# Two more weight slots for the start of a routed expert loop, half of expert 0 ahead of the rest of the gather, and the second group gathered in later units

## What is computed

```python
scores = jax.nn.sigmoid((h @ router_w).astype(f32))
...
gate = jnp.sum(jax.nn.one_hot(top_idx, N_EXPERTS, dtype=f32) * top_w[..., None], axis=1)
...
for e in range(N_EXPERTS):
    he = jax.nn.silu(h @ w_gate[e]) * (h @ w_up[e])
    out = out + gate[:, e:e + 1] * (he @ w_down[e])
```

## Time and profile before

| | |
|---|---|
| median of 3 runs | 921.3 us (921.23 to 923.97) |
| the profiled execution, its own time | 920.35 us |
| its span, first to last instruction | 918.6 us |
| TensorE busy | 816.6 us, 89% of the span |
| VectorE, ScalarE busy | 322.3 us (35%), 181.7 us (20%) |
| mean granted TensorE clock | 0.96 of full speed |
| moved by DMA | 245.87 MB, mean 268 GB/s |

### The profile page before, as it was taken

One profiled execution on the slowest core, in us unless ns is written; L12 is line 12 of the kernel. 1 busy time (PEld: TensorE's weight loads), 2 busy tenths in 40 slices (PEclk: granted clock), 3 DMA queues, 4 the chain that ended last, 5 costly groups with the idle time before them and its releaser, 6 DMA issues. The chain is left out here.

```text
span 918.6 us, 12776 instructions
## 1 busy us (share of the span) xinstructions
PE 816.6 (89%) x5333; PEld 461.7 (50%) x5333; DVE 322.3 (35%) x671; ACT 181.7 (20%) x380; POOL 26.0 (3%) x102
## 2 busy tenths in 40 slices
PE   4999999977999999879579999999599999997882
PEld 3888566535534443323268876654364443432331
DVE  0186456464211111111252964282821111111115
ACT  1143323322211110000121323231241111100001
POOL 7100000000000000000000000000000000000000
PEclk8999999987999999999979999999799999999997
DMA  9744300265899999999935432020858999999991
GB/s 287 270 150 164 128 20 4 89 248 189 351 411 421 421 421 421 421 421 420 393 102 182 155 122 93 2 92 1 366 209 348 423 422 421 421 421 422 419 383 50
DMA packets 54229, 245.87 MB, mean 268 GB/s; under 512 B 8356, under 2 KB 11280, under 8 KB 29584
## 3 DMA queue, kind: packets, MB, share of 16 engines
q1 hardware_dynamic: 49824, 239.41, 65.4%
q0 software_dynamic: 1344, 4.72, 1.5%
q10 hardware_dynamic: 2992, 0.79, 0.4%
HBM read 243.85 MB, written 1.05 MB: 267 GB/s over the span
## 5 line engine op out<-in xcount | busy, mean ns | idle before, releaser
L906 PE MATMUL bank<-x_cm,ring 128*128 128x256 f32 x576 | 130.4, 389 | 6.3 <-ACT x_cm L1878 5.4
L482 PE MATMUL bank<-ring,xg 128*64 128x512 f32 x544 | 124.3, 596 | 10.8 <-DMA ring<-in_exp_w_up 8.6
L482 PE MATMUL bank<-ring_more,xg 128*64 128x512 f32 x480 | 112.5, 611 | 16.5 <-DMA ring_more<-in_exp_w_up 14.5
L906 PEld LDWEIGHTS bank<-x_cm,ring 128*128 128x128 f32 x576 | 112.1, 196 | 23.8 <-ACT x_cm L1878 5.8
L512 PE MATMUL bank<-ring,x_cm 128*64 128x512 f32 x480 | 108.2, 592 | 0.0
L673 DVE TENSOR_TENSOR y_lo<-bank,y_hi 128x512 fp32r<-128x512 f32 x32 | 22.1, 691 | 223.3 <-ACT y_hi L605 223.3
L482 PEld LDWEIGHTS bank<-ring,xg 128*64 128x64 f32 x544 | 40.8, 137 | 78.8 <-issue 73.2
L482 PEld LDWEIGHTS bank<-ring_more,xg 128*64 128x64 f32 x480 | 35.4, 140 | 82.4 <-issue 81.7
L512 PEld LDWEIGHTS bank<-ring,x_cm 128*64 128x64 f32 x480 | 34.8, 137 | 67.2 <-issue 66.3
L605 ACT ACTIVATE y_hi<-bank 128x512 fp32r<-128x512 f32 x32 | 19.1, 598 | 196.2 <-PE bank L512 196.2
L913 PE MATMUL bank<-ring,x_cm 128*128 128x512 f32 x128 | 57.7, 599 | 0.0
(11 more groups left out here) (364 smaller groups left out, 876.7 us busy)
## 6 DMA issues: line engine op xcount, KB each, us to landing
ring<-in_exp_w_down SPq DMA_DIRECT2D x60, 1024.0 KB, 17.6
ring<-in_exp_w_gate SPq DMA_DIRECT2D x34, 1024.0 KB, 13.2
ring<-in_exp_w_up SPq DMA_DIRECT2D x34, 1024.0 KB, 15.3
ring_more<-in_exp_w_gate SPq DMA_DIRECT2D x30, 1024.0 KB, 15.2
ring_more<-in_exp_w_up SPq DMA_DIRECT2D x30, 1024.0 KB, 17.2
ring<-in_w_in SPq DMA_DIRECT2D x24, 1024.0 KB, 9.1
ring<-in_w_out SPq DMA_DIRECT2D x8, 1024.0 KB, 6.5
ring_more<-in_exp_w_down SPq DMA_DIRECT2D x4, 1024.0 KB, 22.4
```

Of the source, the lines that this page charges most:

```text
L482: m = T.matmul(b[SL * i:SL * i + SL, :], xg[g][:, 4 * h + k, cols], w[:, k, :], start=(h == 0 and k == 0), stop=(h == 1 and k == 3))
L906: m = T.matmul(out_, w[:, k, c:c + n], x_cm[:, k, :], start=(k == 0), stop=(k == KD - 1))
```

## The change

`xg[1]`, the gather buffer of the second group, is used as two more slots for weights (`ONCE` = 2) on the first pass round the slots: loads 12 and 13 of a layer, the two halves of expert 1's down matrix, go there. From load 14 on the cycle has its twelve slots again. The landing of these two is counted on an existing semaphore, `rows_loaded`. So that the buffer is free for weights until they are used, the second group is gathered in units 4 to 7, two blocks in each: one where the block stood, and one behind the down product. The slot gates and the pick matrix of the second group move to unit 4. At the start of the expert part only four gather blocks stand ahead of the first half of expert 0 (`first_half`), which is now outside the branch; the other four follow it. For four rounds (not run here) the second group's blocks all stand behind the last unit of a group.

```diff
+    ONCE = 2
...
+    seen, holds, at = [0] * (NSLOT + MORE + ONCE), [None] * (NSLOT + MORE + ONCE), 0
+    for n, (l, name, h, parts) in enumerate(loads):
+        if (name, h) == ("gate0", 0):
+            cycle = [(at + i) % NSLOT for i in range(NSLOT)] + [NSLOT + i for i in range(MORE + ONCE)]
+            at = 0
...
+        at = (at + 1) % len(cycle)
+        if at == 0 and len(cycle) > NSLOT + MORE:
+            cycle = cycle[:NSLOT + MORE]
+        seen[slot] += 16 * len(parts)
...
+        landed.append(seen[slot] if slot < NSLOT + MORE else 16 * (len(rows) + 1 + ONCE * (l + 1)))
...
         def slot_ap(slot):
+            if slot >= NSLOT + MORE:
+                h = slot - NSLOT - MORE
+                return xg[1][:, 4 * h:4 * h + 4, :]
...
+        def steps_of(n, rounds):
+
+            i = n % GU
+            if n + GU >= NE * rounds + i:
+                return (), ()
+            if rounds > 1:
+                return (), tuple(range(KD)) if i == GU - 1 else ()
+            return ((2 * i - KD,), (2 * i - KD + 1,)) if 2 * i >= KD else ((), ())
+
+        def gates_at(n, rounds):
+
+            return n + GU < NE * rounds + n % GU and n % GU == (GU // 2 if rounds == 1 else GU - 1)
...
+        def first_half(pe, l):
+
+            (wg, full_g), (wu, full_u) = slot_w(l, "gate0", 0), slot_w(l, "up0", 0)
+            pe.wait_ge(*full_g)
+            pe.wait_ge(*full_u)
+            for k in range(4):
+                pe.wait_ge(*done("s_first", l, k + 1))
+                for i, w in enumerate((wg, wu)):
+                    T.matmul(b_hid[0][SL * i:SL * i + SL, :], xg[0][:, k, 0:SL], w[:, k, :], start=(k == 0), stop=False)
...
-            pe.wait_ge(*done("s_first", l))
             if rounds == 1:
+                for k in range(4, KD):
+                    pe.wait_ge(*done("s_first", l, k - 3))
+                    inc(gather(k, bank[k % 4], release="t_wgu" if k == 4 else None), "t_first")
                 st.have(pe, "t_gather", GU)
...
-            hidden(0, 0)
...
+            if rounds == 1:
+                pe.wait_ge(*done("s_first", l))
...
-                if g * GU < N:
-                    if n % GU == 0:
+                for k in inside:
+                    if k == 0:
                         pe.wait_ge(*at("v_pick", g + 1))
-                    mark(gather(n % GU, b_hid[n % 2]), "t_gather")
-                    if n % GU == 0:
-                        pe.wait_ge(*at("v_gcol", g))
-                        slot_gates(g)
-                if n + 1 < N:
+                    mark(gather(k, b_hid[n % 2]), "t_gather")
+                    gathered += 1
+                if gates_at(n, rounds) and rounds == 1:
+                    pe.wait_ge(*at("v_gcol", g))
+                    slot_gates(g)
+                turn_of_group = bool(behind) and n % GU == GU - 1
+                if n + 1 < N and not turn_of_group:
                     hidden(n + 1, 0)
...
                 down(n)
+                for k in behind:
...
+                    if rounds == 1 or k > 1:
+                        pe.wait_ge(*at("s_xg", gathered - (rounds > 1)))
+                    mark(gather(k, b_hid[(n + (k if rounds > 1 else 0)) % 2]), "t_gather")
+                    gathered += 1
...
+                if turn_of_group:
+                    hidden(n + 1, 0)
...
-                for k in range(KD):
-                    if k >= 4:
-                        pe.wait_ge(*done("s_first", l, k - 3))
-                    inc(gather(k, bank[k % 4]), "t_first")
+                for k in range(4):
+                    inc(gather(k, bank[k]), "t_first")
+                first_half(pe, l)
                 two_ways(pe, l, lambda rounds: experts_t(pe, l, rounds))
```

More of the change, by code:

```diff
@@ L102, in hybrid_trunk @@
     index = {(l, name, h): n for n, (l, name, h, _) in enumerate(loads)}
[L104 to L118, removed]
     rows, n_rows = {}, 0
@@ L126, in hybrid_trunk @@
         n_rows += L * per
+    slot_of, before, landed = [], [], []
+    seen, holds, at = [0] * (NSLOT + MORE + ONCE), [None] * (NSLOT + MORE + ONCE), 0
[3 more added lines that the diff above has]
+            at = 0
+        elif (name, h) == ("rw0", 0):
+            cycle, at = list(range(NSLOT)), min(range(0, NSLOT, 2), key=lambda b: holds[b]) if l else 0
+        slot = cycle[at]
+        at = (at + 1) % len(cycle)
+        if at == 0 and len(cycle) > NSLOT + MORE:
+            cycle = cycle[:NSLOT + MORE]
+        seen[slot] += 16 * len(parts)
+        slot_of.append(slot)
+        before.append(holds[slot])
+        landed.append(seen[slot] if slot < NSLOT + MORE else 16 * (len(rows) + 1 + ONCE * (l + 1)))
+        holds[slot] = n
     with ExitStack() as ctx:
@@ L395, in two_ways, with gather @@
                     emit(rounds)
-        def gather(k, out_):
+        def gather(k, out_, release=None):
             for j in range(TT):
@@ L473, in hidden @@
                         pe.wait_ge(*at("v_gu", n - 1))
-                    pe.wait_ge(*at("s_xg", min(n + GU if n % GU == 0 else n + GU - 1, N)))
+                    pe.wait_ge(*at("s_xg", GU + sum(len(a) + len(b) for a, b in (steps_of(i, rounds) for i in range(n if n % GU == 0 else n - 1)))))
                 ws = []
@@ L559, in experts_t @@
             inc(m, "t_pos")
+            if rounds == 1:
+                pe.wait_ge(*done("s_first", l))
+            gathered = GU
             for n in range(N):
                 g = n // GU + 1
+                inside, behind = steps_of(n, rounds)
                 hidden(n, 1)
@@ L614, in experts_s @@
             if rounds == 1:
+                for k in range(4, KD):
+                    act.wait_ge(*done("t_first", l, k + 1))
+                    inc(affine_x1(xg[0][:, k, :], bank[k % 4][:], l, k), "s_first")
                 st.have(act, "s_xg", GU)
@@ L624, in experts_s @@
                 silu(n)
-                if n + GU < N:
-                    x_take(n + GU, b_hid[n % 2])
+                inside, behind = steps_of(n, rounds)
+                for k in inside:
+                    x_take((n // GU + 1) * GU + k, b_hid[n % 2])
                 if n == 0:
@@ L629, in experts_s @@
                 y_high(n)
+                for k in behind:
+                    x_take((n // GU + 1) * GU + k, b_hid[(n + (k if rounds > 1 else 0)) % 2])
         def experts_v(dve, l, rounds):
@@ L695, in experts_v @@
                 g = n // GU + 1
-                if n % GU == 0 and g * GU < N:
+                if gates_at(n, rounds) and rounds == 1:
                     picks(g)
@@ L707, in experts_v @@
                 turned_pick(n)
+                if gates_at(n, rounds) and rounds > 1:
+                    picks(g)
+                    gate_col(g)
         def seg_in(q):
@@ L2075, in _ @@
                 inc(A.activation(rt[:, 1], rt[:, 0], ACT.Exp, scale=-1.0), "s_route")
-                for k in range(KD):
+                for k in range(4):
                     act.wait_ge(*done("t_first", l, k + 1))
-                    inc(affine_cm(xg[0][:, k, :], bank[k % 4][:], l, 0, k), "s_first")
+                    inc(affine_x1(xg[0][:, k, :], bank[k % 4][:], l, k), "s_first")
                 two_ways(act, l, lambda rounds: experts_s(act, l, rounds))
```

28 lines of the change are left out of this document (22 added, 6 removed).

## The result

The changed kernel takes **912.6 us** (median of 4 runs, 911.4 to 913.1) against 922.1 (921.2 to 924.0) of the kernel before, run beside it: ratio 0.989, 95% interval 0.987 to 0.991. It is faster, by 9.5 us, where 16.4 were forecast, and 912.6 lies above the forecast range, which ended at 909.0.

The account below looks back on a forecast made before the run. The DMA queue of weight loads was taken to bound the expert part; earlier slot releases bring the last up block 8.2 us earlier a layer, 2 x 8.2 = 16.4 us, from 921.3 to 904.9 us; range 901.5 to 909.0 (8 in 10).

Parts of the forecast that it names:

- What bounds the kernel, and the number per load: Expert part: TensorE stops only for weights queued at the DMA, which brings a load every 2.503 us.
- the load that was named (26): Second half of expert 2, first load again waiting for the one twelve before; issued at 708.28, landing after 6.6 us.
- Two more slots: Start of a layer's loads: 12 and 13 need no release, so two fewer loads behind every release, 5.0 us.
- the sum: Load 26 released 4.93 us earlier, then 67 loads at 2.503; last up block lands 8.2 us earlier a layer.
- First half behind four blocks: Start of the expert part: the 1.11 us wait for ScalarE's eighth copy disappears; load 14 leaves near 672.7.
- the second rival: Branch behind expert 0's first half stalls TensorE on unfetched code; gain only 2.6 us a layer, 916.1; chance 0.04.
- Second group in units 4 to 7: Units 0 to 3 get shorter; units 4 to 7 take 14.4 us, under the DMA's 15.0; nothing new at unit 8.
- The 2.75 and 1.07 us: Time saved without gather blocks and slot gates: 2.75 us in unit 0, 1.07 in each of units 1 to 3.
- What follows load 93 is unchanged: Behind a layer's last up block (load 93): its half, scatter, down and layer norm take the same time.
- the first: Rival: path to load 26 not shortened, relay or row copies surface in units 0 to 3; 912.5; chance 0.10.
- The slower one: Rival: units 4 to 7 take 16.3 us, fall behind the DMA's 15.0, queue stays shallow; 943; chance 0.03.

Follow-up runs that it names:

- early_no_half: early_group with the first half of expert 0 behind eight gather blocks instead of four; 912.0 us.
- early_12: early_group with twelve slots and the first half of expert 0 behind eight gather blocks; 912.0 us.
- early_group: The change with the second group's blocks in units 3 (one), 4 to 6 (two each), 7 (one), expert 8's first half ahead of unit 7's down product; 909.5 us.

## Why the prediction was wrong

*What bounds the kernel, and the number per load.* Right. In the change the load that was named (26) left 45.5 us after the first gather pass (44.9 forecast) and landed after 6.4 us (6.6).

*Two more slots.* Right in kind, too large in size: of the 8.2 us a layer the sum leaves 8.2 - 4.9 = 3.3 for them, and early_no_half against early_12 shows 1.6 and 2.5.

*First half behind four blocks.* Priced at the wait of 1.11 us. The landings of early_group and early_no_half are 1.1 and 1.2 us apart, but landings scatter by more than that among kernels with the same start (219.8 to 221.6 in early_group and its versions with idle products, the same work up to unit 12). The issue of load 26 scatters less: it leaves 45.5 us after the first gather pass in the mean of the eight kernels with two more slots and the early half (45.1 to 45.9), and 46.0 in the four with the late second group and the late half (45.8 to 46.1). That is some 0.6 us a layer, and the missing 0.5 is most of what lies between the 45.5 of load 26 and the 44.9 forecast. The registers and the branch cost nothing. TensorE's sequencer in layer 1 of the change (ns min/median/max, start):

```profile
L401 PEldq COMPARE_BRANCH  x1: 80/80/80, 666.4 to 666.4; - x1
```

It fell through at 666.4, two us ahead of the half's end, and the first gather pass behind it began at 668.35 without a wait. So the second rival is out. The Trainium skill's rule (Runtime: NRT & Kernel Launch, "Instruction fetch mechanics"), that a taken branch to a target outside the fetched code waits for a fetch, agrees with the trace: the jump over the four-round body took 6.16 us at 447.8, again under the layer norm.

*Second group in units 4 to 7.* The 2.75 and 1.07 us came as worked out: units 1 and 2 stand 12.26 us apart (688.43 and 700.69). A unit with two blocks takes 14.8 us rather than 14.4, since a block behind the down product costs 1.38 us (751.78 to 756.60 against 697.25 to 700.69 without one) where one behind the turn costs 1.08. **The step that failed is this one's last:** "The last gather of unit 7 now stands behind the down product, but the wait of 0.97 us before unit 8 exists already, so it costs nothing new". I looked at TensorE's time there and not at SyncE's. The wait is the same, but the half that gives load 58 its slot had moved behind 5.9 us of other work (777.91 to 783.83), and I had followed the release of loads only up to 29. The other side of that step was not seen either: by unit 8 TensorE has done the same work as before and stands at the same place (load 56 leaves 116.3 us after the first gather pass, and 116.5 did before), while the DMA is 8.4 us ahead of where it was (126.8 against 135.2). All that the change wins is taken out of the queue's reserve at unit 8, from 18.7 us to 10.5, and there it met a pause of 12.1. That cost 2.7 us of transfer in layer 0 and 2.9 in layer 1.

*What follows load 93 is unchanged.* The second step that failed, in the profile by 1.7 us a layer: the last half ran mostly at 1.2 GHz in both. The sum had put this at nothing, and so left out what a slow half costs where no wait stands behind it.

The account against the profiled executions: 16.4 forecast, landings 6.2 + 5.2 = 11.4 earlier, less 3.4 for the last halves, gives 8.0; 7.7 were measured. The 5.0 us missing in the landings are no more than the 2.7 + 2.9 = 5.6 us of transfer lost at unit 8. Taking the long pause away brought back 1.2 + 2.2 = 3.4 of them (early_group), less than 5.6 by about what its block in unit 3 cost (1.3 + 0.7). A slip in the sum is too small to matter: a load 26 landed at 714.9 gives load 93 at 882.6, and 882.4 was taken.

*The rivals.* The time came out at that of the first, 912.5, but not by its mechanism: no relay came to the surface in units 0 to 3. The slower one did not occur, since units 4 to 7 at 14.8 us stayed below 15.0, if only just.

## What to carry to other kernels

When a kernel is bound by a stream of loads and each load waits for a slot, moving compute later inside the loop moves slot releases too: follow the releases through the whole loop, and compare each pause between issues with the work that the queue holds at that point, not only at the start. The time to landing of the last load ahead of the pause has to be longer than the pause, and by a margin: here some 5 us, the time that a lone load takes, were enough, and margins under 4 us were not. A gain in a stream is taken from its reserve somewhere, and the place where the reserve is smallest is where to look for the next stall. And once the last wait of a phase is short, what stands behind it counts in full, its clock included.

## What the runs showed of the hardware

TensorE's clock fell to 1.2 GHz after waits as short as 2.1 to 2.4 us, in some halves and not in others with the same wait (before, layer 1: 2.46, 2.42 and 2.42 us ahead of halves of 3.65, 5.35 and 3.65 us), so it is not a matter of the last wait alone. The Trainium skill says (TensorE: Matmul & The Clock Gate, "HAM oscillation — how this bites in real kernels") that bursts of products with DMA waits in between bring the clock down again and again. The runs agree in kind, but the waits of its example are longer, some 3 to 5 us; here 2.1 to 2.4 were enough. In the five kernels with idle products no last half was slow (0 of 10, against 5 of 18 without), and in the four with them in all three units no half of these units was. Where a wait is the DMA's anyway, two products that fit into it bought 2.3 us of 912.6; four that did not fit cost 3.7.
